# A hybrid attention layer on one core: two accumulators in turn for the attention outputs, one bank for the transposed probabilities

## The reference

```python
# A: sliding window of 128, 8 query heads on 2 key/value heads, sinks
s = jnp.where(valid, einsum('bnqhgd,bnkhd->bnhgqk', qb, kb) * scale, -jnp.inf)
m = jnp.maximum(jnp.max(s, -1, keepdims=True), sink)
p = jnp.exp(s - m);  p = p / (jnp.sum(p, -1, keepdims=True) + jnp.exp(sink - m))
o = einsum('bnhgqk,bnkhd->bnqhgd', p, vb)
# B: forgetting attention, 8 heads, causal over all 1024 tokens
s = einsum('bqhd,bkhd->bhqk', qi, k) * scale + ci[..., None] - cum_k[:, :, None, :]
p = jax.nn.softmax(jnp.where(causal, s, -jnp.inf), axis=-1)
o = einsum('bhqk,bkhd->bqhd', p, vf)
```

## Time and profile before

| what | us |
|---|---|
| runs of the kernel (three): median, lowest, highest | 1658.65, 1655.44, 1660.12 |
| the profiled execution: its own time, its span | 1662.93, 1661.1 |
| TensorE busy in the span | 1522.7 (92%) |
| DVE, POOL, ACT busy | 606.9, 603.1, 418.4 |
| mean granted TensorE clock (1 is full speed) | 0.979 |
| attention: first T, last V of step 127 | 208.89 to 533.71 |

### The profile page before, as it was taken

The page is one execution under the profiler, slowest core; times in us unless marked ns, Lnnn a source line. Parts: engine busy times, 40 slices in busy tenths (PEclk is TensorE's granted clock), DMA queues, the critical chain, the costliest instruction groups (busy, mean ns, idle before and its releaser), DMA issues.

```text
span 1661.1 us, 19144 instructions
## 1 busy us (share of the span) xinstructions
PE 1522.7 (92%) x7273; PEld 1239.1 (75%) x7273; DVE 606.9 (37%) x930; ACT 418.4 (25%) x835; POOL 603.1 (36%) x519
## 2 busy tenths in 40 slices
PE   1599979799886899999899999999999999999998
PEld 1488756677665688888768788888888888788886
DVE  4673776655554576566556300000000000002002
ACT  2512056554543210100144300000000000333321
POOL 0501743332413133333112333332333332884860
PEclk9999999899997999999999999999999999999999
DMA  7400021111003534343223221111111111433431
GB/s 287 145 13 0 27 64 36 29 46 51 33 14 88 173 94 126 89 123 104 90 88 135 71 61 51 38 50 51 51 51 44 44 51 38 172 119 127 167 100 51
DMA packets 149674, 132.51 MB, mean 80 GB/s; under 512 B 13200, under 2 KB 130024, under 8 KB 149104
## 3 DMA queue, kind: packets, MB, share of 16 engines
q1 hardware_dynamic: 142960, 123.34, 23.7%
q10 hardware_dynamic: 6656, 8.39, 1.4%
HBM read 119.10 MB, written 12.62 MB: 79 GB/s over the span
## 4 chain that ended last, share of the span: by engine, by line
PE 76%; DVE 11%; ACT 5%; DMA 3%; issue 3%; POOL 2%; SPq 0%; ACTq 0%; DVEq 0%; POOLq 0%
PE PS L1285 64%; PE PS L1361 4%; PE PS L1415 2%; PE PS L1440 1%; DVE s_row L1050 1%; PE PS L1467 1%; POOL s_row L588 1%; ACT p_a L715 1%; PE PS L1468 1%; DMA xin<-in_x_dram 1%; DMA woraw<-in_w_out_dram 1%; DVE mx L1031 1%; ACT pt_hi L731 1%; PE PS L1296 1%; DVE rope_b L1000 1%
## 5 line engine op out<-in xcount | busy, mean ns | idle before, releaser
L1285 PE MATMUL PS<-act_hi,w_hi 128*128 128x512 f32 x960 | 375.4, 391 | 1.9 <-DVE ostage L1080 1.9
L1285 PE MATMUL PS<-act_hi,w_lo 128*128 128x512 f32 x960 | 374.2, 390 | 0.0
L1285 PE MATMUL PS<-act_lo,w_hi 128*128 128x512 f32 x960 | 374.1, 390 | 0.0
L1285 PEld LDWEIGHTS PS<-act_hi,w_hi 128*128 128x128 f32 x960 | 180.5, 188 | 39.2 <-issue 2.0
L1285 PEld LDWEIGHTS PS<-act_hi,w_lo 128*128 128x128 f32 x960 | 180.6, 188 | 37.9
L1285 PEld LDWEIGHTS PS<-act_lo,w_hi 128*128 128x128 f32 x960 | 180.7, 188 | 37.2
L550 POOL TENSOR_TENSOR scratch<-ones 128x1 f32<-128x1 f32 x68 | 13.4, 197 | 528.7 <-PE PS L1285 462.6
L559 POOL TENSOR_TENSOR w_lo<-wraw,w_hi 128x1024 fp32r<-128x1024 f32 x81 | 202.4, 2498 | 6.5
L1261 DVE TENSOR_TENSOR act_ff<-PS,sl 128x512 f32 x40 | 27.7, 692 | 407.6 <-PE PS L1285 407.6
L1285 PE MATMUL PS<-w_hi,ah_hi 128*128 128x512 f32 x352 | 137.0, 389 | 2.2 <-POOL w_lo L649 2.2
L1285 PE MATMUL PS<-w_lo,ah_hi 128*128 128x512 f32 x352 | 136.9, 389 | 0.0
(11 more groups left out here) (217 smaller groups left out, 2524.3 us busy)
## 6 DMA issues: line engine op xcount, KB each, us to landing
wraw<-in_w_ffn_in_dram SPq DMA_DIRECT2D x44, 512.0 KB
w2raw<-in_w_ffn_out_dram SPq DMA_DIRECT2D x44, 512.0 KB, 3.4
adaraw<-in_w_ada_dram SPq DMA_DIRECT2D x32, 512.0 KB, 4.0
wraw<-in_w_in_dram SPq DMA_DIRECT2D x25, 512.0 KB
wada<-in_w_ada_dram SPq DMA_DIRECT2D x4, 2048.0 KB, 9.7
xin<-in_x_dram SPq DMA_DIRECT2D x8, 512.0 KB, 10.2
cs<-ncum_dram SPq DMA_DIRECT2D x4, 1024.0 KB, 4.6
merged<-oT_dram ACTq DMA_DIRECT2D x8, 512.0 KB, 7.2
```

The source lines that it names most:

```text
L1285: ins = nc.tensor.matmul(out_ap, lhs[a], rhs[b], start=first and i == 0, stop=last and i == 2)
```

## The change

Bank 5 changes sides. The transposes always go to bank 4, so T of step gp + 1 now waits for `group_lo` of step gp. The outputs of tasks and units go to bank 6 and bank 5 in turn, so the first V of a unit waits for the read-out of the unit before the last one. On every engine the instructions, their number and their order stay as they were; only banks and wait counts differ.

```diff
-                nc.scalar.activation(pt_hl[gp % 3][0][:, 0:n], PS[:, 4 + gp % 2, 0:n], ACT.Copy).then_inc(grp_hi, 1)
+                nc.scalar.activation(pt_hl[gp % 3][0][:, 0:n], PS[:, 4, 0:n], ACT.Copy).then_inc(grp_hi, 1)
...
-                    nc.scalar.activation(stage[0:HALF, :], PS[HALF:P, 6], ACT.Copy).then_inc(o_half, 1)
+                    nc.scalar.activation(stage[0:HALF, :], PS[HALF:P, 6 - u % 2], ACT.Copy).then_inc(o_half, 1)
...
-                nc.vector.tensor_tensor(pt_hl[gp % 3][1][:, 0:n], PS[:, 4 + gp % 2, 0:n],
+                nc.vector.tensor_tensor(pt_hl[gp % 3][1][:, 0:n], PS[:, 4, 0:n],
...
-                    nc.vector.tensor_tensor(stage[half, :], PS[half, 6], stage[half, :], ALU.add).then_inc(o_taken, 1)
+                    nc.vector.tensor_tensor(stage[half, :], PS[half, 6 - u % 2], stage[half, :], ALU.add).then_inc(o_taken, 1)
...
             def transpose_p(gp):
-                if gp < 2:
-                    pe.wait_ge(proj_taken, 9 + gp)
+                if gp == 0:
+                    pe.wait_ge(proj_taken, 9)
                 else:
-                    pe.wait_ge(grp_lo, gp - 1)
+                    pe.wait_ge(grp_lo, gp)
...
-                        ins = nc.tensor.transpose(PS[:, 4 + gp % 2, (i - i0) * P:(i - i0 + 1) * P],
+                        ins = nc.tensor.transpose(PS[:, 4, (i - i0) * P:(i - i0 + 1) * P],
                                                   s_row[i][:, h, kb * P:(kb + 1) * P], ident[:, :])
...
             def times_v(gp):
                 if (h if is_a else kb) == 0:
-                    if u == 0:
-                        pe.wait_ge(proj_taken, 7)
+                    if u < 2:
+                        pe.wait_ge(proj_taken, 7 + 3 * u)
                     else:
-                        pe.wait_ge(o_taken, u)
+                        pe.wait_ge(o_taken, u - 1)
                 pe.wait_ge(grp_lo, gp + 1)
...
-                    whole = PS[:, 6, c0:c0 + m]
+                    whole = PS[:, 6 - u % 2, c0:c0 + m]
```

More of the change, by code:

```diff
@@ L739, in out_half @@
                 if u < A_T:
-                    nc.scalar.activation(stage[0:HALF, 0:2 * P], PS[HALF:P, 6, 0:2 * P], ACT.Copy)
-                    nc.scalar.activation(stage[HALF:P, 0:2 * P], PS[0:HALF, 6, 2 * P:4 * P], ACT.Copy).then_inc(o_half, 1)
+                    nc.scalar.activation(stage[0:HALF, 0:2 * P], PS[HALF:P, 6 - u % 2, 0:2 * P], ACT.Copy)
+                    nc.scalar.activation(stage[HALF:P, 0:2 * P], PS[0:HALF, 6 - u % 2, 2 * P:4 * P], ACT.Copy).then_inc(o_half, 1)
                 elif u % 2 == 0:
-                    nc.scalar.activation(stage[0:HALF, :], PS[HALF:P, 6], ACT.Copy).then_inc(o_half, 1)
+                    nc.scalar.activation(stage[0:HALF, :], PS[HALF:P, 6 - u % 2], ACT.Copy).then_inc(o_half, 1)
                 else:
-                    nc.scalar.activation(stage[HALF:P, :], PS[0:HALF, 6], ACT.Copy).then_inc(o_half, 1)
+                    nc.scalar.activation(stage[HALF:P, :], PS[0:HALF, 6 - u % 2], ACT.Copy).then_inc(o_half, 1)
             def out_send(u):
@@ L1075, in out_add @@
                 if u < A_T:
-                    nc.vector.tensor_tensor(stage[0:HALF, 0:2 * P], PS[0:HALF, 6, 0:2 * P], stage[0:HALF, 0:2 * P], ALU.add)
-                    nc.vector.tensor_tensor(stage[HALF:P, 0:2 * P], PS[HALF:P, 6, 2 * P:4 * P], stage[HALF:P, 0:2 * P], ALU.add)                        .then_inc(o_taken, 1)
+                    nc.vector.tensor_tensor(stage[0:HALF, 0:2 * P], PS[0:HALF, 6 - u % 2, 0:2 * P], stage[0:HALF, 0:2 * P], ALU.add)
+                    nc.vector.tensor_tensor(stage[HALF:P, 0:2 * P], PS[HALF:P, 6 - u % 2, 2 * P:4 * P], stage[HALF:P, 0:2 * P], ALU.add)                        .then_inc(o_taken, 1)
                 else:
                     half = slice(0, HALF) if u % 2 == 0 else slice(HALF, P)
-                    nc.vector.tensor_tensor(stage[half, :], PS[half, 6], stage[half, :], ALU.add).then_inc(o_taken, 1)
+                    nc.vector.tensor_tensor(stage[half, :], PS[half, 6 - u % 2], stage[half, :], ALU.add).then_inc(o_taken, 1)
             def log_gates():
@@ L1433, in transpose_p @@
                             c = (2 * b + pl) * P
-                            ins = nc.tensor.transpose(PS[:, 4 + gp % 2, c:c + P], p_a[t % 3][:, 2 * h + pl, b * P:(b + 1) * P],
+                            ins = nc.tensor.transpose(PS[:, 4, c:c + P], p_a[t % 3][:, 2 * h + pl, b * P:(b + 1) * P],
                                                       ident[:, :])
```

## The result

| | before | changed |
|---|---|---|
| median of the runs side by side (4 each), us | 1659.24 | 1677.05 |
| lowest and highest | 1655.44, 1660.12 | 1676.15, 1677.86 |
| the profiled execution, own time and span | 1662.93, 1661.1 | 1676.15, 1674.1 |

The changed kernel is slower: ratio 1.0089, 95% interval 1.0070 to 1.0108. On 1659.24 that is 14.8 us (11.6 to 17.9). The two medians differ by 17.8 us, a ratio of 1.0107, which lies at the upper end of that interval. The recorded ratio can't be worked out again from the medians above; it is what I use for every kernel, and the loss is to be read as 15 to 18 us. The forecast was 9.7 us, with a range of 1660.5 to 1677.

What follows compares the result with a forecast made beforehand. The prediction took branch A as bound by its chain without TensorE, the middle by TensorE, and the last sixteen steps, once changed, by the ring. 0.3 + 2.1 + 0.0 + 7.3 = 9.7 us, giving 1668.4 us, range 1660.5 to 1677.

Steps and rivals of the forecast that it cites:

- the ring: Attention steps: with one bank, T waits for `pt_lo`, that for `pt_hi`, that for T; no step under 2.00 us.
- One sign that I had named for being wrong: The forecast would be wrong if, among other signs, the granted clock in the last pair differed; no size given.
- Branch A: Its chain goes round without TensorE, so both edits bring nothing; +0.3 us for the passage into branch B.
- The middle: Branch B, pairs one to three: three full steps at 2.00 for 1.82 us, +0.7 us a pair, +2.1 in all.
- The last pair: Branch B's last pair: first eight steps at nothing, last sixteen turn wholly into the ring, +7.3 us.
- The term of the clock: Last sixteen steps: clock at half until about 520 us, four T of four at 0.46 us more each, +1.9 us.
- the third rival: The clock stays low in the last pair and into the gates: +15.6 us, 1674.2; chance 0.12 shared with branch A slowing.
- the case I called likeliest: The prediction's own forecast for the whole kernel, +5 to +13 us; chance 0.67.
- the one on branch A: Branch A's ring goes through V: 0.35 us in each of 16 tasks, +5.6, 1674.0 us; chance 0.12 shared with low clock.
- The read-outs: V no longer waits for the output bank's read-out: 0.2 us back once a middle pair, nothing in the last pair.
- That the accumulators decide: Rival: all waits for read-outs come back and T finds its bank free, 11.8 us faster, 1646.9; chance 0.07.
- Cancelling: Rival: last pair costs only 5.4, units' first V gain 3.2, middle +1.6; +3.8 us, 1662.5; chance 0.14.

Runs made afterwards that it cites:

- E6: The kernel before with a single transpose bank in branch A alone (steps 0 to 31), one accumulator throughout; ratio 1.0003, +0.5 us.
- E7: The kernel before with a single transpose bank in the first three pairs of branch B alone (steps 32 to 103); ratio 1.0033, +5.5 us.
- E3: The kernel before with a single transpose bank from step 104 on alone, one accumulator throughout; ratio 1.0077, +12.8 us.
- E4: The changed kernel with three bf16 matmuls that nobody reads ahead of the transposes of steps 112 to 127; ratio 1.0063, +10.5 us against the kernel before.
- E2: The changed kernel, but with two transpose banks in turn from step 104 on, beside the two accumulators; ratio 1.0024, +4.0 us against the kernel before.
- E1: The changed kernel's single transpose bank, but all outputs in one bank with the old read-out wait; ratio 1.0130, +21.6 us against the kernel before.
- E9: E1 with three bf16 matmuls that nobody reads in each of steps 105 to 126; ratio 1.0079, +13.1 us against the kernel before.
- E10: The changed kernel with three bf16 matmuls that nobody reads in each of steps 105 to 126; ratio 1.0063, +10.5 us against the kernel before.
- E5: The kernel before with two transpose banks everywhere and a second accumulator for the last pair alone; ratio 0.9990, -1.7 us.

## Why the prediction was right and where not

**The direction and the mechanism** were right, and the size of the ring's loss was put too low. T goes behind `pt_lo`, the ring replaces TensorE's own pace, and it holds in exactly the places named: not in branch A (E6), a little in the middle (E7), wholly in the last sixteen steps (E3). One sign that I had named for being wrong did come: the granted clock in the last pair differed. And the number lies at an end of the range: the ratio on the forecast's base of 1658.65 gives 1673.4 us against 1668.4, the median is 1677.05 against an upper bound of 1677.

**Branch A** was forecast at +0.3 us with the passage into branch B, and measured at -0.2. The passage lies in the next row, and there T of the steps 33 to 37 keeps its distance from T of step 32 within 0.1 us. The slack before `pt_hi` took the delay, as argued.

**The middle** was forecast at +2.1 us and came to +4.0 from T to T. Of that, 0.45 us is the delayed T of step 104 itself; the V of step 104 stands 3.55 us later, against V of step 32. The term mis-sized is the turn of the ring, 2.00 us in the forecast and 2.07 measured. I had taken T at 0.60 us, as the earlier trace rows show it for a T that did not wait; a T that has waited takes 0.66, and 0.06 us pass before it starts. The difference per step grows from 0.18 to 0.24 or 0.25. The second mis-sizing is the number of turns: in each pair of the middle V falls back by 0.21 to 0.25 us in four steps in a row, and I had counted three.

**The last pair** was forecast at +7.3 us and came to +11.2 in its sixteen steps. Two terms of the sum were too small. The ring at full clock was put at +5.4; with the clock held up by E4's filling the part takes 29.8 us, +7.0. From T of step 112 to the end of the last `pt_lo` E4 takes 29.3 us where the sum had 27.7: its T add up to 9.6 us in place of 8.3 (0.66 in place of 0.60 for four, and 1.09 for the first, which still ran at the lower clock), and the joints make up the rest. The term of the clock was put at +1.9, and 34.0 less 29.8 makes it 4.2 us. I had the lower clock end at 520 us, as before the change, with four transposes of 0.46 us more; the changed kernel spent 23.7 us of the part at half of the full clock, not 9.0.

This was the third rival, at 15.6 us for both its pieces. The measured +14.8 us lies next to it, and beyond the 5 to 13 us of the case I called likeliest; I had given it 0.12 together with the one on branch A. That the totals lie so close is in part luck. The rival adds 4.2 us in the last pair and 1.7 us after it, a price that no row of mine showed, and leaves the rest of the sum alone. The profiles have 2.3 us more for the clock in the last pair and at most 1.0 after it, the ring is 1.6 us dearer there and the middle 1.9, and the eight steps before give 1.6 back.

The Trainium skill, in the section of TensorE: Matmul & The Clock Gate that the prediction cites (a kernel that cycles its banks, with idle times between groups of matmuls), would have made this rival the likely one. By the windows above the trace agrees on the idle times and on a clock that goes between both levels. It doesn't bear out the cycling as the reason: the transposes of the changed kernel stay in one bank, with 23.7 us low, where before they took two in turn, with 9.0, and E2, with two of each in turn there, had 5.7.

**The read-outs** were put at 0.2 us a pair and nothing in the last pair. That part is the least settled. E1 says that the second accumulator gives back 6.8 us (2.6 to 11) of what the single transpose bank costs, E9 and E10 say 2.6 us once the clock is mostly held. 1.0 us of the first and 1.4 of the second is in the middle. How much of the rest is the freed V of step 104, and how much is that the clock falls early without it (at 493.9 us in E1 and 491.4 in E9, at 497.7 in the changed kernel), the runs don't tell apart. The early fall isn't due to the banks of the last pair: E7, which has two transpose banks there, has it too, 2.8 us after T of step 104, where E1 and E9 have it after 2.4 and 2.5 us and the changed kernel, E2, E3 and E4 after 10 or 11. It came only where the middle had one transpose bank and one accumulator.

**After attention** I expected nothing. The span has +1.0 us there, with 4.3 us more at the low clock; E9 and E10 with 22.4 and 18.7 us low are 2.0 us shorter than before in this part, E2 and E5 with 28.8 and 28.9 us are 2.5 and 2.6 us longer. So its length goes roughly with its time at the low clock, over one execution each, and I can't tie it to a step.

**The rivals.** That the accumulators decide fell with the measurement, and E1 and E5 price them: 6.8 us (2.6 to 11) beside a single transpose bank, and none that shows in the time beside two (-1.7 us, -3.8 to +0.5). Cancelling fell with the measurement: in the profiles nothing but the eight steps came back, and those 1.6 us stand beside 4.3 us less of low clock.

## What to carry to other kernels

When two buffers compete for one spare bank, compare the rings that each closes: write, read, read again, write. The bank belongs to the one whose ring is longer than what the engine has to do between two writes, step by step, and not to the one with the larger sum of waits today. A wait that isn't there yet must be read from how far the later instruction starts ahead of the event it would wait for. And a stretch that goes from busy to half idle may lose the clock as well as the wait, so price it at both levels.

## What was not expected of the hardware

Transposes that waited on a semaphore took 0.66 us for four where those that did not wait took 0.60, and started 0.06 us after the end of what they waited for. At the low clock it was 1.11 against 1.05 to 1.09.

Matmuls whose result nobody reads made the last sixteen steps shorter. Three of 512 columns in each turn of the ring, with 0.28 us of idle time left of 2.07 in E4's rows, kept the full clock from 520 to 545 us (1.00 in the window in E4 and in E10), where the changed kernel had 0.52 from 528 to 542. In the time that was 14.8 down to 10.5 us, with overlapping intervals; over the last sixteen steps it was 34.0 down to 29.8.
